# Long convolution on one core: the signal folded twice, and fewer weight tiles for its transform

## The chip, the cores and the metric

The kernel runs on one core of a Trainium2 chip. The metric is the device time of one launch in microseconds (us), the median of several executions. Five engines work side by side, each on its own list of instructions: TensorE (PE, matrix products), VectorE (DVE), ScalarE (ACT), GpSimd (POOL) and SyncE (SP, which issues most DMAs). They meet at semaphores only.

## The reference

The reference is a two-layer language model block (gated recurrence, windowed attention, feed-forward) followed by a second two-layer block on the same 512 positions and 1024 channels (latent attention, then a "hyena" layer). The change is in the hyena layer, whose core is a long convolution by Fourier transform:

```python
def fft_long_conv(u, spec):
    L = u.shape[1]                                  # 512 positions
    U = jnp.fft.rfft(u.astype(jnp.float32), n=2 * L, axis=1)
    return jnp.fft.irfft(U * spec, n=2 * L, axis=1)[:, :L].astype(u.dtype)

def hyena_seq(t, w_in, conv_w, conv_b, spec, bias, w_out):
    u, gate = jnp.split(t @ w_in, [(HY_ORDER + 1) * HY_WIDTH], axis=-1)
    u = depthwise_conv(u, conv_w, conv_b)           # width 3
    v, *gates = jnp.split(u, HY_ORDER + 1, axis=-1)
    z = v
    for o in range(HY_ORDER):                       # 2 convolutions
        z = gates[o] * (fft_long_conv(z, spec[:, o]) + z * bias[o])
    return (z * jax.nn.silu(gate)) @ w_out
```

`spec` is the spectrum of a filter that is computed from small weights, once per launch.

## The kernel before

**Precision and weights.** Every product is made of three matmuls of the fast float type: high part by high part, high by low, low by high (`mm_w`, lines 322 to 328; `mm_x` at 330 with the operands exchanged). A tile is one 128x128 piece of a weight matrix; with 512 columns of data it costs three matmuls (L324, L327, L328). All weights of the launch come as one stream of chunks, 8 tiles each (512 KB). For each chunk SP loads `raw`, ACT writes the high part `whi` (L1196) and DVE the low part `wlo` (L1879). There are 4 buffers of `raw` and 3 of `whi` and `wlo` (`RAW, HL = 4, 3`).

**Where the splits stand.** The tiles are counted in order by `Tiles.take` on TensorE and by `Ahead.tiles` (L1173) in the programs of ACT and DVE. When the count passes the seventh tile of chunk c (`self.n % 8 == 6`), ACT and DVE place the split of chunk c + 2 at that point of their own lists. So the number of tiles that a stage takes sets not only TensorE's work but also *between which of their other instructions* ACT and DVE make the splits of that stage and of all stages behind it. TensorE waits for the `wlo` of a chunk at the chunk's first tile.

**The hyena layer** (from about 1640 us of the span on) works on halves of the channels, c = 0 and 1 (4 blocks `ct` of 128 channels each), and on two convolutions, od = 0 and 1. The order is: projections (`channels`), turn(0,0), convolve(0,0), projections and turn(1,0), convolve(1,0), projections of the second half and turn(0,1), convolve(0,1), projections and turn(1,1), convolve(1,1), output projection. Pairs in brackets are (od, c).

- `turn(od, c)` folds the signal in time. DVE writes, for each block ct, the sum and the difference of positions t and 511 - t (L2590 and L2592, 256 columns each) to `zf`. TensorE transposes 16 pieces of `zf` (L1035), four at a time (t = 0 to 3); each group of four reads all four blocks, so the first group waits for DVE's last fold. ACT and DVE take each group out as `zh` (L1774) and `zl` (L2597). This is woven into the projections by fixed counts (`weave`), the same counts on all engines.
- `convolve(od, c)` has four steps `forward(j)`, one for each group of 128 frequencies, and four `inverse(j)`, in the order forward 0, forward 1, inverse 0, forward 2, inverse 1, forward 3, inverse 2, inverse 3. A forward takes two tiles for the filter's real part (PSUM bank `bk`), two for its imaginary part (`bj`), for j = 0 two more (`alt`), then two for the signal's real part (`bu`, from the sums) and two for its imaginary part (`bi`, from the differences): 10 tiles for j = 0, 8 for the others. The signal's tiles are those named `mdft`.
- Behind each forward DVE makes four products (L2617, L2620, L2621, L2624), POOL the difference of the first two (L2782) and DVE the sum of the others (L2626); ACT takes the high parts (`yh`, L1816), DVE the low parts (`yl`, L2629). An inverse takes 4 tiles with half the columns (24 matmuls at L331, L334, L335) and waits for `yl`.
- For j = 0 ACT and DVE mend row 0 of the filter's spectrum (L1809, then `hl_h` at L2611), and forward(1) waits for it on TensorE (`made_v "hm"`, line 1069).
- Behind inverse(3) DVE makes four results of each of four blocks (L2650, L2651, L2654, L2657) and only then the next split.

The lines of `convolve` on TensorE that take the signal's tiles:

```python
for k in range(2):
    w = tiles.take([("mdft", k, j)])
    ...
    op = mm_w(bu, w, a.zh[:, k, :], a.zl[:, k, :], k == 0, k == 1)
op.then_inc(*s.filled.tick("bu", od, c, j))
```

Of the kernel before, what the change touches and what calls it, by code (L numbers as in the profile page):

```python
# [13 lines left out]
MUL, ADD, SUB = ALU.mult, ALU.add, ALU.subtract  # L14
# [300 lines left out]
def tensor_program(e, m, s):  # L315
    q = Waits(e)
# [653 lines left out]
    def hyena():  # L970
        a = m.hy
# [83 lines left out]
        def convolve(od, c):  # L1055
            y = a.y[od, c]
            bu, bk, bi, bj = B[4:8]
            prev = (0, c) if od else (1, 0) if c else None

            def forward(j):  # L1060
                sums, differences = (0, 1), (2, 3)
                for k, x in enumerate(sums if j < 2 else differences):
                    w = tiles.take([("dft", k, j)])
                    if k == 0:
                        if j:
                            q.wait_ge(*s.taken_a.at("bk", od, c, j - 1))
                        else:
                            q.wait_ge(*(s.taken_a.at("bk", *prev, 3) if prev else s.h.at("mla_out", 2)))
                        q.wait_ge(*(s.made_v.at("hm", od, c) if j else s.made_v.at("h_lo", od, c, 0)))
                    op = mm_w(bk, w, a.hh[:, 0, x, :], a.hl[:, 0, x, :], k == 0, k == 1)  # L1070
                op.then_inc(*s.filled.tick("bk", od, c, j))
                for k, x in enumerate(differences if j < 2 else sums):
                    w = tiles.take([("dft", k, 4 + j)])
                    if k == 0:
                        q.wait_ge(*(s.taken_a.at("bj", od, c, j - 1) if j else s.made_v.at("zt", od, c, 3)))
                        q.wait_ge(*s.made_v.at("h_lo", od, c, 3))
                    op = mm_w(bj, w, a.hh[:, 1, x, :], a.hl[:, 1, x, :], k == 0, k == 1)
                op.then_inc(*s.filled.tick("bj", od, c, j))
                if j == 0:
                    for k, x in enumerate(sums):  # L1080
                        w = tiles.take([("alt", k, 0)])
                        if k == 0:
                            q.wait_ge(*s.taken_a.at("bk", od, c, 0, "first"))
                        op = mm_w(bk, w, a.hh[:, 0, x, :], a.hl[:, 0, x, :], k == 0, k == 1)
                    op.then_inc(*s.filled.tick("alt", od, c))
                for k in range(2):
                    w = tiles.take([("mdft", k, j)])
                    if k == 0 and j:
                        q.wait_ge(*s.taken_v.at("bu", od, c, j - 1))
                    elif k == 0:  # L1090
                        q.wait_ge(*(s.taken_v.at("bu", *prev, 3) if prev else s.h.at("mla_out", 1)))
                    op = mm_w(bu, w, a.zh[:, k, :], a.zl[:, k, :], k == 0, k == 1)
                op.then_inc(*s.filled.tick("bu", od, c, j))
                for k in range(2):
                    w = tiles.take([("mdft", k, 4 + j)])
                    if k == 0 and j:
                        q.wait_ge(*s.taken_v.at("bi", od, c, j - 1))
                    op = mm_w(bi, w, a.zh[:, 2 + k, :], a.zl[:, 2 + k, :], k == 0, k == 1)
                op.then_inc(*s.filled.tick("bi", od, c, j))

            def inverse(j):
                i = j % 2
                for p in range(2):
                    hi, lo, old = tiles.take([("idft", j, 2 * p + x) for x in range(2)])
                    half = slice(256 * p, 256 * p + 256)
                    q.wait_ge(*s.made_v.at("y_lo", od, c, j, p))
                    for ct in range(4):
                        cs = slice(128 * ct, 128 * ct + 128)
                        if j == 0 and p == 0:
                            if od == 0:  # L1110
                                q.wait_ge(*s.taken_a.at("conv", 8 + 4 * c + ct))
                            elif ct < 2:
                                q.wait_ge(*s.taken_a.at("conv", 16 + 4 * c + ct + 2))
                            else:
                                q.wait_ge(*s.taken_v.at("hg", c, ct))
                        op = mm_x(B[ct][:, half], (hi, lo), y.hi[:, i, p, cs], y.lo[:, i, p, cs], j == 0 and p == 0,
                                  j == 3, old if ct == 0 else None, skip=True)
                        if j == 3 and p == 1 and ct < 3:
                            op.then_inc(*s.valued.tick("inv", od, c, ct))
                op.then_inc(*s.valued.tick("ydone", od, c, j))  # L1120

            forward(0)
            for j in range(1, 4):
                forward(j)
                if j == 3 and (od, c) != (1, 1):
                    for x in range(2):
                        tiles.mark(("rows", *((0, 1) if od else (1, c)), x), x)
                inverse(j - 1)
            inverse(3)
            if od == 1 and c == 1:  # L1130
                for gen in begun:
                    for _ in range(4):
                        next(gen)
# [53 lines left out]
def scalar_program(e, m, s, A, chunks):  # L1187
    q = Waits(e)
# [9 lines left out]
    w = Ahead(split_hi, chunks)  # L1198
# [519 lines left out]
    def hyena():  # L1718
        a = m.hy
# [57 lines left out]
        def convolve(od, c):  # L1777
            y = a.y[od, c]
            bu, bk, bi, bj = B[4:8]
            ks, tmp = m.sqb, a.tmp  # L1780

            def forward(j):
# [16 lines left out]
                if j == 0:  # L1799
# [7 lines left out]
                    e.activation(a.alt[:, :], bk, ACT.Copy).then_inc(*s.taken_a.tick("bk", od, c, 0))  # L1807
                    q.wait_ge(*s.made_v.at("row 0", od, c))
                    e.activation(a.hh[0:1, 0, 0, :], a.hm[0:1, :], ACT.Copy).then_inc(*s.made_a.tick("hm", od, c))  # L1809
                for _ in range(4):  # L1810
                    w.tiles(1)
                for p, name in enumerate(("yr", "spec")):
                    q.wait_ge(*(s.made_v if p else s.made_p).at(name, od, c, j))
# [58 lines left out]
def vector_program(e, m, s, chunks):  # L1872
    q = Waits(e)
# [671 lines left out]
    def hyena():  # L2545
        a = m.hy
# [39 lines left out]
        def turn(od, c):  # L2586
            zf = a.zf[2 * c + od]
            for ct in range(4):
                q.wait_ge(*(s.made_v.at("inv", 0, c, ct) if od else s.made_v.at("conv", 4 * c + ct)))
                e.tensor_tensor(zf[:, ct, 0:256], z[:, ct, 0:256], z[:, ct, 511:255:-1],  # L2590
                                ADD).then_inc(*s.made_v.tick("zf0", od, c, ct))
                e.tensor_tensor(zf[:, ct, 256:512], z[:, ct, 0:256], z[:, ct, 511:255:-1],  # L2592
                                SUB).then_inc(*s.made_v.tick("zf", od, c, ct))
                yield
            for t in range(4):
# [4 lines left out]
        def convolve(od, c):  # L2600
# [3 lines left out]

            def forward(j):
                i = j % 2
                for _ in range(10 if j == 0 else 8):
                    w.tiles(1)
                if j == 0:
                    q.wait_ge(*s.made_a.at("hm", od, c))  # L2610
# [324 lines left out]
def fourier():  # L2935
# [14 lines left out]
    ic[0, :] = 1 / 1024  # L2950
    isn[0, :] = -alt / 1024
    cat = lambda a, b: np.concatenate([a, b], 1).astype(np.float32)
    return cat(c, s), c2.astype(np.float32), cat(mc, ms), cat(ic, isn)


def filter_tables():
# [131 lines left out]
```

## Time and profile before

| what | value |
|---|---|
| median of 3 runs | 2037.94 us (2037.1 to 2038.3) |
| span of the profiled execution | 2037.5 us, 0.4 us below the median |
| PE busy | 1978.4 us, 97% |
| DVE busy | 1380.5 us, 68% |
| ACT busy | 828.0 us, 41% |
| mean granted clock of TensorE | 0.988 of full |

TensorE is busy nearly all the time, so its idle stretches and the number of its matmuls tell most of the time. The busy share of DVE is a mean: in the hyena layer it is higher in some stretches than in others, and there it can be what TensorE waits for. A matmul's duration in the trace is its latency; the distance between two starts is its cost in a row of them.

### The profile page before, as it was taken

To read this page: it belongs to the slowest core of one execution; us is meant where nothing else is said; L and a number is where in the kernel's file an instruction comes from. 1 tells how busy PE (TensorE), PEld (TensorE's weight loads), DVE (VectorE), ACT (ScalarE), POOL (GpSimd) and SP (SyncE) were. 2 spreads that over 40 slices of the span, in tenths; PEclk is the share of its full clock that TensorE was granted. 3 is DMA by queue.
4 is the path that set the end of the run, shared out by engine and by line. 5 is a ranking of instruction groups with operands and counts; after the bars stand their busy time and mean duration, and the time that the engine had idled before them with its cause. 6 is when DMAs were issued, how large, how long until landed. Compare 5 with 4: busy or idle time off the path is not lost.

```text
span 2037.5 us, 24678 instructions
## 1 busy us (share of the span) xinstructions
PE 1978.4 (97%) x9878; PEld 1655.8 (81%) x9878; DVE 1380.5 (68%) x1961; ACT 828.0 (41%) x1259; POOL 233.3 (11%) x234
## 2 busy tenths in 40 slices
PE   8999999999999999999999999999999989999997
PEld 6888887788888888888888888778888878888786
DVE  5577765997789667756764784555555567787774
ACT  5233334442233245544432443444344444454442
POOL 2132231003201230010000001000000101000011
PEclk9999999999999999999999999999999989999998
DMA  5211112345534341114344333311111323232421
GB/s 182 72 56 54 61 53 85 130 150 179 201 138 157 132 137 34 40 64 147 137 159 135 126 133 99 108 62 42 42 32 42 114 73 124 93 126 81 145 94 52
DMA packets 60963, 208.40 MB, mean 102 GB/s; under 512 B 6832, under 2 KB 7152, under 8 KB 59696
## 3 DMA queue, kind: packets, MB, share of 16 engines
q1 hardware_dynamic: 53296, 193.19, 27.9%
q10 hardware_dynamic: 7552, 13.64, 1.9%
q8 instruction: 78, 1.28, 0.2%
q14 instruction: 37, 0.30, 0.0%
HBM read 196.31 MB, written 10.49 MB: 101 GB/s over the span
## 4 chain that ended last, share of the span: by engine, by line
PE 79%; DVE 13%; ACT 5%; issue 2%; POOL 1%; DMA 0%; ACTq 0%; DVEq 0%; SPq 0%
PE PS L324 21%; PE PS L328 20%; PE PS L327 20%; DVE wlo L1879 2%; PE PS L436 2%; PE PS L933 2%; PE PS L331 1%; PE PS L335 1%; PE PS L334 1%; ACT whi L1196 1%; PE PS L922 1%; PE PS L685 1%; PE PS L386 1%; PE PS L726 1%; DVE col_f L2094 1%
## 5 line engine op out<-in xcount | busy, mean ns | idle before, releaser
L324 PE MATMUL PS<-nhi,whi 128*128 128x512 f32 x1456 | 593.1, 407 | 15.4 <-DVE wlo L1879 3.7
L328 PE MATMUL PS<-nhi,wlo 128*128 128x512 f32 x1456 | 571.8, 393 | 0.0
L327 PE MATMUL PS<-nlo,whi 128*128 128x512 f32 x1456 | 570.6, 392 | 0.0
L1879 DVE TENSOR_TENSOR wlo<-raw,whi 128x1024 fp32r<-128x1024 f32 x291 | 368.4, 1276 | 176.5 <-ACT whi L1196 175.4
L1196 ACT ACTIVATE whi<-raw 128x1024 fp32r<-128x1024 f32 x291 | 303.3, 1052 | 209.0 <-PE PS L324 133.2
L324 PEld LDWEIGHTS PS<-nhi,whi 128*128 128x128 f32 x1456 | 276.1, 190 | 78.4 <-issue 11.3
L328 PEld LDWEIGHTS PS<-nhi,wlo 128*128 128x128 f32 x1456 | 275.3, 189 | 59.7
L327 PEld LDWEIGHTS PS<-nlo,whi 128*128 128x128 f32 x1456 | 276.4, 190 | 53.5 <-issue 2.6
L2723 POOL TENSOR_TENSOR diag<-diag,sqb 128x512 f32<-128x512 f32 (+1 forms) x56 | 73.6, 1314 | 780.9 <-ACT sqb L1205 698.3
L324 PE MATMUL PS<-hh_f,whi 128*128 128x512 f32 x352 | 137.8, 392 | 0.0
L327 PE MATMUL PS<-hl_f,whi 128*128 128x512 f32 x352 | 137.7, 391 | 0.0
L328 PE MATMUL PS<-hh_f,wlo 128*128 128x512 f32 x352 | 137.5, 391 | 0.0
L2739 POOL TENSOR_TENSOR sd_f<-ab_f 128x512 f32<-128x512 f32 x32 | 55.3, 1745 | 271.7 <-DVE ab_f L2182 271.1
L2094 DVE SCALAR_TENSOR_TENSOR col_f<-aw_f,scv,col_f 128x1024 f32<-128x1024 f32 x63 | 85.0, 1358 | 0.0
L328 PEld LDWEIGHTS PS<-hh_f,wlo 128*128 128x128 f32 x352 | 66.5, 189 | 14.0
L324 PEld LDWEIGHTS PS<-hh_f,whi 128*128 128x128 f32 x352 | 66.4, 189 | 13.9
L327 PEld LDWEIGHTS PS<-hl_f,whi 128*128 128x128 f32 x352 | 66.5, 189 | 13.7
L1419 ACT ACTIVATE t_f<-gp_f,par 128x512 f32<-128x512 f32 x44 | 35.9, 816 | 94.3 <-DVE gp_f L2199 94.3
L1665 ACT ACTIVATE pt_m<-PS 128x768 f32<-128x768 f32 x32 | 25.9, 811 | 111.8 <-PE PS L922 111.8
L1923 DVE TENSOR_TENSOR hT<-hT,PS 128x512 f32<-128x512 f32 x48 | 32.8, 682 | 52.2 <-PE PS L328 52.1
L436 PEld LDWEIGHTS PS<-qa,kk 128*128 128x128 f32 x448 | 56.0, 191 | 14.2 <-DVE qa L2031 10.3
L1205 ACT ACTIVATE sqb<-hT 128x512 f32<-128x512 f32 x42 | 26.3, 629 | 94.7 <-DVE hT L1923 62.5
(356 smaller groups left out, 3373.2 us busy)
## 6 DMA issues: line engine op xcount, KB each, us to landing
raw<-in_stream SPq DMA_DIRECT2D x291, 512.0 KB, 3.5
aw_f<-in_ada SPq DMA_DIRECT2D x48, 512.0 KB, 4.4
rows<-sd_f ACTq DMA_DIRECT2D x32, 256.0 KB, 2.2
rows_h<-rows SPq DMA_DIRECT2D x8, 1024.0 KB, 6.1
wd_f<-in_decay ACTq DMA_DIRECT2D x16, 256.0 KB, 3.0
hT<-in_xT SPq DMA_DIRECT2D x8, 256.0 KB, 6.9
out<-hT SPq DMA_DIRECT2D x8, 256.0 KB, 2.0
wd_f<-in_filt_out ACTq DMA_DIRECT2D x8, 128.0 KB, 2.9
```

The costliest lines, as they stand in the source:

```text
L324: op = e.matmul(out, hi, xh, start=first, stop=False)
L327: e.matmul(out, hi, xl, start=False, stop=False)
L328: return e.matmul(out, lo, xh, start=False, stop=last)
L436: op = e.matmul(B[b][:, cs], kk[:, z, cs], qx[:, cs], start=True, stop=True)
L933: op = e.matmul(B[6][:, 128 * blk:128 * blk + 128], a.v[:, t, 128 * h:128 * h + 128], a.pt[:, i, 128 * t:128 * t + 128], start=t == 0, sto ...
L1196: e.activation(m.whi[:, c % HL, :], m.raw[:, c % RAW, :], ACT.Copy).then_inc(*s.w_hi.tick(c))
L1419: e.activation(a.t[:, 0, z, :], a.gp[:, z, 2:T + 2], ACT.Identity, bias=pc(cb, f), scale=pc(cw, 44 + f)).then_inc(*s.made_a.tick("c0", lay ...
L1879: e.tensor_tensor(m.wlo[:, c % HL, :], m.raw[:, c % RAW, :], m.whi[:, c % HL, :].bitcast(F), SUB).then_inc(*s.w_lo.tick(c))
L1923: op = e.tensor_tensor(h, h, B[b], ADD)
L2094: e.scalar_tensor_tensor(col[:, v, :], aw[:, n % AW[layer], :], m.scv[:, 2, k, v:v + 1], col[:, v, :], MUL, ADD).then_inc(*s.made_v.tick(" ...
L2723: e.tensor_tensor(acc, acc, m.sqb[:, i % 2 if site != "n4" else 0, 0:width], ADD).then_inc(*s.acc.tick(site, i))
L2739: e.tensor_tensor(a.sd[:, x, :], a.ab[:, 0, :], a.ab[:, 1, :], SUB if x else ADD).then_inc(*s.made_p.tick("sd", n, i, x))
```

## The change

The time-folded signal (256 rows of sums, 256 of differences) is folded once more, about the middle of its 256 rows. Of the four frequency groups the first two (every fourth frequency from 0, and from 2) have cosines and sines that are even or odd about that middle, so one half of the rows' contribution vanishes. For j = 0 and j = 1 the real and the imaginary part of the signal then take one tile each and not two. For j = 2 and 3 nothing is saved. The matrix `mdft` is folded on the host in the same way and scaled by 1/2. On DVE each block ct of a turn has two folds more: the first pair writes `zs` (in the buffer `sqb`), and a second pair, which waits for the first, writes `zf`.

```diff
+Z_SIGNS = [((0,), (1,)), ((1,), (0,)), ((0, 1), (0, 1)), ((0, 1), (0, 1))]
+Z_TILES = [2, 2, 4, 4]
...
-                for k in range(2):
+                for k in even:
                     w = tiles.take([("mdft", k, j)])
...
+                    op = mm_w(bu, w, a.zh[:, k, :], a.zl[:, k, :], k == even[0], k == even[-1])
...
-                for k in range(2):
+                for k in odd:
                     w = tiles.take([("mdft", k, 4 + j)])
...
-                for _ in range(4):
+                for _ in range(Z_TILES[j]):
                     w.tiles(1)
...
-                e.tensor_tensor(zf[:, ct, 0:256], z[:, ct, 0:256], z[:, ct, 511:255:-1],
+                e.tensor_tensor(zs[:, 0:256], z[:, ct, 0:256], z[:, ct, 511:255:-1],
+                                ADD).then_inc(*s.made_v.tick("zs0", od, c, ct))
+                e.tensor_tensor(zs[:, 256:512], z[:, ct, 0:256], z[:, ct, 511:255:-1],
+                                SUB).then_inc(*s.made_v.tick("zs1", od, c, ct))
+                q.wait_ge(*s.made_v.at("zs1", od, c, ct))
+                e.tensor_tensor(zf2[:, :, 0, :], zs2[:, :, 0:128], zs2[:, :, 255:127:-1],
                                 ADD).then_inc(*s.made_v.tick("zf0", od, c, ct))
-                e.tensor_tensor(zf[:, ct, 256:512], z[:, ct, 0:256], z[:, ct, 511:255:-1],
+                e.tensor_tensor(zf2[:, :, 1, :], zs2[:, :, 0:128], zs2[:, :, 255:127:-1],
                                 SUB).then_inc(*s.made_v.tick("zf", od, c, ct))
...
-                for _ in range(10 if j == 0 else 8):
+                for _ in range(Z_TILES[j] + (6 if j == 0 else 4)):
                     w.tiles(1)
...
+    folded = lambda a: np.concatenate([(a[0:128] + a[255:127:-1]) / 2, (a[0:128] - a[255:127:-1]) / 2], 0)
+    return cat(c, s), c2.astype(np.float32), cat(folded(mc), folded(ms)), cat(ic, isn)
```

A convolution thus takes 46 tiles and not 50, the launch 289 chunks and not 291. Counted from convolve(0,0), which starts at the first tile of a chunk, the four convolutions start at tile 0, 2, 4 and 6 of a chunk before the change and at 0, 6, 4 and 2 after it.

The first place where instructions move is turn(1,1) on DVE, in the projections ahead of the last convolution. `zf<-z_h` is a fold, `sqb<-z_h` and `zf<-sqb` are the first and second folds of the new code, `wlo` is the split of a chunk. Before:

```order
L1879 TENSOR_TENSOR wlo<-raw,whi 128x1024
L2590 TENSOR_TENSOR zf<-z_h 128x256
L2592 TENSOR_TENSOR zf<-z_h 128x256
L2590 TENSOR_TENSOR zf<-z_h 128x256
L2592 TENSOR_TENSOR zf<-z_h 128x256
L2580 SCALAR_TENSOR_TENSOR rb<-rb,PS 128x512
L2583 SCALAR_TENSOR_TENSOR g_h<-g_h,rb 128x512
L1879 TENSOR_TENSOR wlo<-raw,whi 128x1024
```

The same place after the change:

```order
L2599 TENSOR_TENSOR sqb<-z_h 128x256
L2601 TENSOR_TENSOR sqb<-z_h 128x256
L2604 TENSOR_TENSOR zf<-sqb 128x2x128
L2606 TENSOR_TENSOR zf<-sqb 128x2x128
L1882 TENSOR_TENSOR wlo<-raw,whi 128x1024
L2599 TENSOR_TENSOR sqb<-z_h 128x256
L2601 TENSOR_TENSOR sqb<-z_h 128x256
L2604 TENSOR_TENSOR zf<-sqb 128x2x128
L2606 TENSOR_TENSOR zf<-sqb 128x2x128
L2583 SCALAR_TENSOR_TENSOR rb<-rb,PS 128x512
L2586 SCALAR_TENSOR_TENSOR g_h<-g_h,rb 128x512
```

Each block has four folds now, and the split stands between the first and the second block, where it stood ahead of both before.

The second place is DVE at the start of convolve(1,1). `rb` and `g_h` are the last gate of the projections, `hl_h` is the mended row. Before:

```order
L2580 SCALAR_TENSOR_TENSOR rb<-rb,PS 128x512
L2583 SCALAR_TENSOR_TENSOR g_h<-g_h,rb 128x512
L1879 TENSOR_TENSOR wlo<-raw,whi 128x1024 x2
L2611 TENSOR_TENSOR hl_h<-rb,hh_h 1x512
L2617 TENSOR_TENSOR tmp_h<-PS,sqb 128x512
```

After:

```order
L2583 SCALAR_TENSOR_TENSOR rb<-rb,PS 128x512
L2586 SCALAR_TENSOR_TENSOR g_h<-g_h,rb 128x512
L1882 TENSOR_TENSOR wlo<-raw,whi 128x1024
L2625 TENSOR_TENSOR hl_h<-rb,hh_h 1x512
L2631 TENSOR_TENSOR tmp_h<-PS,sqb 128x512
```

One split stands ahead of the mended row and not two; the other has moved behind the step's products.

## Rows read from the trace of the kernel before

**Rows 1.** What TensorE waited for, 1655 us to the end: total us, times, longest
```profile
PE PS L331 <- DVE yl L2629: 4.3, 4, 1.5
PE PS L324 <- DVE hl_h L2611: 2.8, 2, 1.4
PE PS L324 <- DVE wlo L1879: 2.8, 2, 2.1
```

**Rows 2.** Timeline of TensorE, convolve(0,0): start, us, engine, line, operation [idle before]
```profile
1693.46 0.39 PE L324 MATMUL PS<-zh_h,whi 128*128 128x512 f32 x1
...
1695.95 0.39 PE L328 MATMUL PS<-zh_h,wlo 128*128 128x512 f32 x1
1697.78 0.47 PE L324 MATMUL PS<-hh_h,whi 128*128 128x512 f32 x1 [1.44 <-DVE hl_h L2611]
...
1720.02 0.28 PE L331 MATMUL PS<-whi,yh 128*128 128x256 f32 x1
...
1722.77 0.28 PE L335 MATMUL PS<-whi,yl 128*128 128x256 f32 x1
```

**Rows 3.** Timeline of VectorE, turn(0,0), and two results behind convolve(0,0)
```profile
1671.00 0.42 DVE L2590 TENSOR_TENSOR zf<-z_h 128x256 f32<-128x256 f32 x1
1671.33 0.42 DVE L2592 TENSOR_TENSOR zf<-z_h 128x256 f32<-128x256 f32 x1
...
1675.93 0.42 DVE L2592 TENSOR_TENSOR zf<-z_h 128x256 f32<-128x256 f32 x1
...
1727.16 0.41 DVE L2651 TENSOR_TENSOR tmp_h<-PS,sqb 128x256 f32<-128x256 f32 x1
1727.61 0.75 DVE L2654 SCALAR_TENSOR_TENSOR tmp_h<-z_h,par,tmp_h 128x512 f32<-128x512 f32 x1
```

**Rows 4.** Timeline of all engines, ends of the four turns: last folds, first transposes
```profile
1677.26 0.60 PE L1035 MATMUL PS<-ident,zf 128*128 128x128 f32 x4
...
1755.01 0.65 PE L1035 MATMUL PS<-ident,zf 128*128 128x128 f32 x4
...
1844.60 0.75 DVE L2557 SCALAR_TENSOR_TENSOR tmp_h<-up_h,par,tmp_h 128x512 f32<-128x512 f32 x1 [0.75 <-ACT tmp_h L1740]
...
1846.50 0.69 PE L1035 MATMUL PS<-ident,zf 128*128 128x128 f32 x4
...
1917.03 0.69 DVE L2580 SCALAR_TENSOR_TENSOR rb<-rb,PS 128x512 f32<-128x512 f32 x1 [0.75 <-ACT rb L1763]
...
1920.51 0.42 DVE L2592 TENSOR_TENSOR zf<-z_h 128x256 f32<-128x256 f32 x1
1921.65 0.60 PE L1035 MATMUL PS<-ident,zf 128*128 128x128 f32 x4
```

**Rows 5.** Timeline of VectorE, the first step of convolve(0,0)
```profile
1697.56 0.67 DVE L2617 TENSOR_TENSOR tmp_h<-PS,sqb 128x512 f32<-128x512 f32 x1
1698.16 0.67 DVE L2620 TENSOR_TENSOR tmp_h<-PS,sqb 128x512 f32<-128x512 f32 x1
...
1700.89 1.29 DVE L2629 TENSOR_TENSOR yl<-tmp_h,yh 128x512 fp32r<-128x512 f32 x2
1703.37 1.23 DVE L1879 TENSOR_TENSOR wlo<-raw,whi 128x1024 fp32r<-128x1024 f32 x1 [1.18 <-ACT whi L1196]
1704.51 0.68 DVE L2617 TENSOR_TENSOR tmp_h<-PS,sqb 128x512 f32<-128x512 f32 x1
```

**Rows 6.** Timeline, last step of convolve(1,1), and TensorE behind convolve(0,1)
```profile
1901.11 0.50 PE L324 MATMUL PS<-nhi,whi 128*128 128x512 f32 x1 [2.05 <-DVE wlo L1879]
...
1971.48 0.68 DVE L2620 TENSOR_TENSOR tmp_h<-PS,sqb 128x512 f32<-128x512 f32 x1
...
1974.97 0.39 PE L331 MATMUL PS<-whi,yh 128*128 128x256 f32 x1 [1.55 <-DVE yl L2629]
```

**Rows 7.** Stretches: PE, PEld, DVE, ACT, POOL busy (x), PEclk, DMA share, GB/s
```profile
1322.00:1324.00 2.00, 0.21 (x1) 0.24 (x2) 0.79 (x2) 2.00 (x5) 0.57 (x1) 1.00 0.00 0
1572.00:1574.00 2.00, 1.08 (x3) 0.89 (x4) 1.97 (x5) 0.00 (x0) 0.00 (x0) 0.50 0.00 0
```

More of the change, by code:

```diff
@@ L1085, in forward @@
                     op.then_inc(*s.filled.tick("alt", od, c))
-                for k in range(2):
-                    w = tiles.take([("mdft", k, j)])
[L1088 to L1092, printed above, removed]
+                even, odd = Z_SIGNS[j]
+                if j:
+                    q.wait_ge(*s.taken_v.at("bu", od, c, j - 1))
+                else:
+                    q.wait_ge(*(s.taken_v.at("bu", *prev, 3) if prev else s.h.at("mla_out", 1)))
+                for k in even:
+                    w = tiles.take([("mdft", k, j)])
+                    op = mm_w(bu, w, a.zh[:, k, :], a.zl[:, k, :], k == even[0], k == even[-1])
                 op.then_inc(*s.filled.tick("bu", od, c, j))
-                for k in range(2):
+                if j:
+                    q.wait_ge(*s.taken_v.at("bi", od, c, j - 1))
+                for k in odd:
                     w = tiles.take([("mdft", k, 4 + j)])
-                    if k == 0 and j:
-                        q.wait_ge(*s.taken_v.at("bi", od, c, j - 1))
-                    op = mm_w(bi, w, a.zh[:, 2 + k, :], a.zl[:, 2 + k, :], k == 0, k == 1)
+                    op = mm_w(bi, w, a.zh[:, 2 + k, :], a.zl[:, 2 + k, :], k == odd[0], k == odd[-1])
                 op.then_inc(*s.filled.tick("bi", od, c, j))
@@ L2588, in turn @@
             for ct in range(4):
+                zs = m.sqb[:, ct % 2, :]
+                zs2, zf2 = zs.rearrange("p (a t) -> p a t", a=2), zf[:, ct, :].rearrange("p (a b t) -> p a b t", a=2, b=2)
                 q.wait_ge(*(s.made_v.at("inv", 0, c, ct) if od else s.made_v.at("conv", 4 * c + ct)))
-                e.tensor_tensor(zf[:, ct, 0:256], z[:, ct, 0:256], z[:, ct, 511:255:-1],
+                if od == 0 and c == 0:
+                    q.wait_ge(*s.sums.at("n5"))
+                elif ct < 2:
+                    q.wait_ge(*s.made_v.at("inv", *((0, c) if od else (1, 0)), 3))
+                e.tensor_tensor(zs[:, 0:256], z[:, ct, 0:256], z[:, ct, 511:255:-1],
[4 more added lines that the diff above has]
+                e.tensor_tensor(zf2[:, :, 0, :], zs2[:, :, 0:128], zs2[:, :, 255:127:-1],
                                 ADD).then_inc(*s.made_v.tick("zf0", od, c, ct))
-                e.tensor_tensor(zf[:, ct, 256:512], z[:, ct, 0:256], z[:, ct, 511:255:-1],
+                e.tensor_tensor(zf2[:, :, 1, :], zs2[:, :, 0:128], zs2[:, :, 255:127:-1],
                                 SUB).then_inc(*s.made_v.tick("zf", od, c, ct))
@@ L2952, in fourier @@
     cat = lambda a, b: np.concatenate([a, b], 1).astype(np.float32)
-    return cat(c, s), c2.astype(np.float32), cat(mc, ms), cat(ic, isn)
+    folded = lambda a: np.concatenate([(a[0:128] + a[255:127:-1]) / 2, (a[0:128] - a[255:127:-1]) / 2], 0)
+    return cat(c, s), c2.astype(np.float32), cat(folded(mc), folded(ms)), cat(ic, isn)
 def filter_tables():
```

## The prediction, on record before the kernel ran

> **What bounds the kernel now.** I read the list of TensorE's waits first, because TensorE is busy nearly throughout: whatever it does not wait for costs only what its own matmuls cost. In the hyena layer it waits 4.3 us in four waits for `yl`, 2.8 us in two for `hl_h`, 2.8 us in two for `wlo` [rows 1]: each time for VectorE. Then the timeline of TensorE in one convolution, for the price of a tile: from 1693.46 to 1695.95 lie 11 distances between matmul starts, 0.226 us each, so a tile (three matmuls) costs 0.68 us [rows 2]. Then VectorE's timeline in the turns and in the steps of a convolution, to see how much room it has. In the turns it has little; that decides the case.
>
> **Removed on TensorE.** Two tiles in forward(0) and two in forward(1), four convolutions: 16 tiles, 16 x 0.68 = 10.9 us if TensorE alone set the pace. With them go two chunks, with their loads and splits; nothing waited for the loads, and the splits' time is within what follows.
>
> **Added on VectorE, the turns.** A pair of folds is 0.33 us from start to start, 1671.00 to 1671.33 [rows 3]. The second pair waits for the first's last result. What such a wait costs stands at L2651 to L2654: 0.45 us from start to start where 0.33 would do, so 0.12 more [rows 3]. A block gets 2 x 0.33 + 0.12 = 0.79 us more, a turn 4 x 0.79 = 3.2 us. The new form (2 x 128 columns, read backwards) is not in this trace. The nearest row is the old fold, also 256 columns with one operand backwards, and I take it; the upper bound is the pitch of an instruction of 512 columns, 0.60 us from 1697.56 to 1698.16 [rows 5], which would make 8 x 0.27 = 2.1 us more in a turn, 8.5 us in all. A gain is excluded, as the elements are no fewer.
>
> TensorE's first transposes read the last fold, so I take off the room of each turn:
> - turn(0,0): the last fold ends at 1675.93 + 0.42 = 1676.35; the fourth transpose, which reads it, starts a quarter us behind 1677.26 [rows 3, 4]. Room 1.2, new wait 2.0 us.
> - turn(1,0): its splits now fall as those of turn(1,1) did before, since its projections start at the same tile of a chunk (the sixth). There the last fold ends at 1920.93 and the fourth transpose starts at 1921.9: room 1.0, and VectorE stood idle 0.75 us among the folds at 1917.03 [rows 4]. New wait 3.2 - 1.0 - 0.75 = 1.4 us.
> - turn(0,1): same order as before. Its four transposes take 0.69 us where those of 1677.26 take 0.60: they wait already. Idle 0.75 at 1844.60 [rows 4]. New wait 2.4 us.
> - turn(1,1): takes the order that turn(1,0) had. There the transposes at 1755.01 take 0.65 us, so they wait already [rows 4], and VectorE works without a gap of note from the end of the convolution on. New wait 3.2 us.
>
> Together 9.0 us of new waits. Behind the transposes stand the matmuls of the projections in TensorE's list, so nothing fills them. Later waits do not absorb them either: the whole chain to `hl_h` starts from TensorE's own `alt` product.
>
> **Moved: the split behind a convolution.** VectorE makes 16 results behind inverse(3) before the next split. Where the convolution ends at the sixth tile of a chunk, TensorE has 10 tiles of cover and then waits: 2.05 us at 1901.11, behind convolve(0,1) [rows 6]. Convolutions ended at tile 2, 4, 6, 0 of a chunk, and now end at 6, 4, 2, 0. The wait moves from convolve(0,1) to convolve(0,0): +2.05 - 2.05 = 0.
>
> **The convolutions.** Two tracks run side by side. TensorE's, from the release by `hl_h`: 6 tiles of forward(1), then twice an inverse (24 matmuls from 1720.02 to 1722.77, so 2.9 us [rows 2]) and 8 tiles. VectorE's: a step of products, sum and low parts is 4.6 us from 1697.56 to the end of `yl` at 1702.18, and each split adds 1.15 us [rows 5] and, where ScalarE makes the high half behind its `yh`, 0.2 to 1.2 us of waiting. At the end stands a fixed chain, L2620 at 1971.48 to inverse(3) at 1974.97, 3.5 us [rows 6]. I laid both tracks with the new order of the splits:
> - convolve(0,0): TensorE waited 1.44 us for `hl_h` at 1697.78 [rows 2], and the chain to `hl_h` starts ahead of the signal's tiles. So forward(0)'s two tiles (1.36 us) only lengthen the wait. Forward(1)'s 1.36 is gained, and 0.6 of the last wait, because no split stands ahead of the last products now: 2.0.
> - convolve(1,0): `hl_h` has no split just ahead of it and comes 6.1 us behind the start; TensorE is ready at 5.4 and waits 0.7. After that TensorE sets the pace: 1.9.
> - convolve(0,1): the same start; in the last step two splits stand ahead of the products, which come 0.6 us later than TensorE: 1.3.
> - convolve(1,1): VectorE and ScalarE also make `nlo` and `nhi`. Forward(1) starts 1.8 us earlier (one split less ahead of `hl_h`, as the second order piece shows), but VectorE's steps then last 7.5, 7.1 and 8.6 us, as long as before, and the last wait grows from 1.55 to some 3.2 us: 1.4.
>
> Gained together 6.6 us of the 10.9. The bounds of this term are 2 x 1.36 = 2.7 us (only the two forwards(1) in which nothing but TensorE worked) and 10.9 us.
>
> **The clock.** TensorE now waits five times for 2.7 to 3.2 or for 2.0 to 2.4 us. The trace shows both outcomes: an idle stretch of that size at 1322 us with the granted clock at 1.00, and 0.50 (1.2 GHz where 1.00 is 2.4 GHz) at 1572 us behind two idle stretches [rows 7]. A fall costs half of the time for which it lasts while TensorE is the bound. I take one fall that costs 1.2 us; bounds 0 and 5. The Trainium skill (TensorE: Matmul & The Clock Gate, Why this matters for your kernels) says the same of idle gaps between bursts of matmuls, as a rule against making them; the trace agrees at 1572 us and not at 1322 us. [...]
>
> **Sum.** The profiled execution spans 2037.5 us: + 9.0 - 6.6 + 0 + 1.2 = + 3.6, that is 2041.1. The median of the runs lies 0.4 above it: 2041.5 us. I call 0.2% (4.1 us, to 2033.9 and 2042.0) the bound below which a measurement of this kernel tells no change. So: no change, but close to slower.
>
> **Rivals.**
> 1. Slower by the clock: the new waits of 2.0 to 3.2 us, all in front of stretches where TensorE is the bound, bring its clock down three or four times. Against it speaks the stretch at 1322 us, of the same size, which left the clock at 1.00 [rows 7]. From two falls on the kernel is measurably slower; with four, 5 us: 2037.9 + 2.4 + 5 = 2045.3. Chance 0.2.
> 2. No fall of the clock: 2037.9 + 9.0 - 6.6 = 2040.3. Chance 0.3.
> 3. The convolutions give all of the 10.9 us, as TensorE's share of busy time suggests: 2037.9 + 9.0 - 10.9 = 2036.0. Against it: four waits for `yl` and two for `hl_h` show that VectorE's track is already the longer one at places. Chance 0.1.
> 4. Faster: the folds find room that I do not see and the turns cost nothing. 2037.9 - 10.9 = 2027.0, or 2031.3 with 6.6. Against it: the transposes wait already in two turns of four. Chance 0.05.
> 5. The new form of fold costs like 512 columns: 8.5 more, 2050. Chance 0.03, since columns set the time in all rows of VectorE that I read.
>
> The forecast itself has 0.32. Range: 2037.5 to 2045. Below it lie rivals 3 and 4, above it 5. Slower than 2042.0 are rivals 1 and 5 nearly whole and four tenths of the forecast's own scatter (1.5 us to either side): 0.38. Faster than 2033.9: rival 4 and a little of 3: 0.06. Within: 0.56.
>
> **What would show it.** In the changed kernel TensorE's waits list a new entry, transposes (L1035) behind VectorE's second folds, four times, some 9 us together and over 3 us the longest. The wait for `wlo` of 2 us stands behind convolve(0,0) and not (0,1). The wait for `yl` ahead of the last inverse of convolve(1,1) is near 3 us. A second fold is 0.33 us behind the one ahead of it. The waits for `hl_h` are 2.8 us in convolve(0,0) and below 1 in the others. The slices of the granted clock show whether it fell behind 1690 us. The prediction is wrong if the transposes wait less than 6 us together, or if the hyena layer's convolutions are shortened by over 9 us.

## The result, and the profile after

The changed kernel takes 2045.54 us (median of 5 runs, 2045.26 to 2045.86), the kernel before 2037.89 us beside it (5 runs, 2035.19 to 2038.3): ratio 1.0036, 95% interval 1.0023 to 1.0048. It is slower, by 7.7 us. The forecast was 2041.5 us, its range ended at 2045.0, and "slower" had a chance of 0.38.

The list of TensorE's waits from 1655 us on in the changed kernel (total us, times, longest), against [rows 1]:

```profile
PE PS L1037 <- DVE zf L2606: 7.6, 6, 2.3
PE PS L333 <- DVE yl L2643: 5.4, 4, 2.7
PE PS L326 <- DVE hl_h L2625: 5.0, 4, 2.8
PE PS L326 <- DVE wlo L1882: 2.8, 2, 2.1
```

The transposes are new in the list with 7.6 us. The waits for `hl_h` grew from 2.8 to 5.0 us and those for `yl` from 4.3 to 5.4; those for `wlo` are as they were. Where they stand is in the timeline of TensorE (start, us, operation [idle before <- releaser]), picked rows of the changed kernel:

```profile
1675.13 0.33 PE L1037 MATMUL PS<-ident,zf 128*128 128x128 f32 x1 [0.49 <-DVE zf L2606]
1676.60 0.33 PE L1037 MATMUL PS<-ident,zf 128*128 128x128 f32 x1 [1.14 <-DVE zf L2606]
...
1698.41 0.76 PE L326 MATMUL PS<-hh_h,whi 128*128 128x512 f32 x1 [2.79 <-DVE hl_h L2625]
...
1736.88 0.50 PE L326 MATMUL PS<-nhi,whi 128*128 128x512 f32 x1 [2.05 <-DVE wlo L1882]
...
1851.16 0.33 PE L1037 MATMUL PS<-ident,zf 128*128 128x128 f32 x1 [2.21 <-DVE zf L2606]
...
1924.64 0.33 PE L1037 MATMUL PS<-ident,zf 128*128 128x128 f32 x1 [0.31 <-DVE zf L2606]
1927.25 0.48 PE L1037 MATMUL PS<-ident,zf 128*128 128x128 f32 x1 [2.27 <-DVE zf L2606]
...
1979.80 0.38 PE L333 MATMUL PS<-whi,yh 128*128 128x256 f32 x1 [2.70 <-DVE yl L2643]
```

These are turns (0,0), (0,1) and (1,1), `hl_h` and `wlo` in and behind convolve(0,0), and `yl` ahead of the last inverse. Turn (1,0) has a wait of 1.14 us at 1759.09. The wait for `wlo` that stood at 1901.11 [rows 6] now stands at 1736.88. The last row answers to the 1.55 us at 1974.97 [rows 6].

The folds themselves, VectorE's timeline of the changed kernel in turn(0,0), against [rows 3]:

```profile
1668.00 0.42 DVE L2599 TENSOR_TENSOR sqb<-z_h 128x256 f32<-128x256 f32 x1
1668.34 0.42 DVE L2601 TENSOR_TENSOR sqb<-z_h 128x256 f32<-128x256 f32 x1
1668.79 0.43 DVE L2604 TENSOR_TENSOR zf<-sqb 128x256 f32<-128x256 f32 x1
1669.13 0.42 DVE L2606 TENSOR_TENSOR zf<-sqb 128x256 f32<-128x256 f32 x1
```

The new form costs what the old one does: 0.42 us, starts 0.34 us apart and 0.45 where it waits for the one ahead (0.33 and 0.45 in [rows 3]).

Then the granted clock, read in stretches of 2 us from 1650 to 1995 us. Busy times stand first, the clock (PEclk) is the third number from the end; five places of the changed kernel:

```profile
1676.00:1678.00 2.00, 1.40 (x6) 1.17 (x7) 2.00 (x4) 0.60 (x1) 0.00 (x0) 0.87 0.00 0
1678.00:1680.00 2.00, 2.00 (x6) 1.42 (x5) 1.70 (x3) 0.00 (x0) 0.00 (x0) 0.50 0.47 131
1680.00:1682.00 2.00, 2.00 (x10) 1.81 (x9) 0.29 (x1) 0.92 (x2) 0.00 (x0) 0.78 0.32 131
1698.00:1700.00 2.00, 1.59 (x4) 1.33 (x5) 2.00 (x5) 0.00 (x0) 0.46 (x1) 0.50 0.66 147
1852.00:1854.00 2.00, 2.00 (x7) 1.50 (x6) 0.84 (x2) 0.12 (x1) 0.00 (x0) 0.50 0.32 43
1928.00:1930.00 2.00, 2.00 (x6) 1.60 (x5) 1.14 (x2) 1.51 (x3) 0.00 (x0) 0.50 0.32 129
1982.00:1984.00 2.00, 2.00 (x12) 2.00 (x11) 0.33 (x1) 0.00 (x0) 0.00 (x0) 0.50 0.34 53
```

Each place stands at one of the waits above: of 1.14 (with 0.49 us just ahead), 2.79, 2.21, 2.27 and 2.70 us. The clock falls between 0.6 us ahead of the wait's end (at 1926.6, where the wait ends at 1927.25) and 1.5 us behind it (at 1981.3, where it ends at 1979.80). What a fall costs is worked out from the first three rows: 2 x (0.13 + 0.50 + 0.22) = 1.7 us of TensorE's time. All stretches below 1.00 between 1650 and 1995 us together make 8.5 us, five times 1.7. I call this sum the clock's loss. It is an upper bound of what the falls cost, since two of them begin while TensorE still waits, which is some 0.5 us of the 8.5. In the trace of the kernel before the loss is 0; three long stretches of it:

```profile
1690.00:1727.00 37.00, 34.30 (x194) 29.79 (x194) 27.25 (x38) 17.31 (x28) 5.17 (x4) 1.00 0.33 113
...
1811.00:1860.00 49.00, 48.26 (x220) 39.56 (x219) 38.38 (x54) 24.99 (x34) 0.00 (x0) 1.00 0.32 103
...
1897.00:1945.00 48.00, 45.95 (x211) 37.74 (x210) 34.92 (x48) 23.07 (x32) 0.00 (x0) 1.00 0.29 90
```

The account: 16 tiles, -10.9; transposes, +7.6; `hl_h`, +2.2; `yl`, +1.1; clock, +8.5. Sum +8.5 us, where the medians differ by 7.7. The two traces themselves differ by 9.2 us from turn(0,0)'s first fold to the end: 366.5 us (from 1671.00, span 2037.5) and 375.7 us (from 1668.00, span 2043.7). Ahead of that fold the code is the same, and yet the changed kernel was 3.0 us quicker there, with 13.7 us of loss between 400 and 1650 us against 18.8.

So the clock also falls where nothing was changed, and not in each execution. One place shows it best: near 1323 us TensorE waits 2.63 us for VectorE in all 14 profiled kernels of this document, with the same code up to there. In 10 of them, the kernel before among them, the clock stays at 1.00; in four (e2, e4, e9 and e11 below) it falls. Here are e9's rows:

```profile
1324.01 0.76 PE L325 MATMUL PS<-nhi,whi 128*128 128x512 f32 x1 [2.63 <-DVE call L2378]
1324.00:1326.00 2.00, 1.99 (x5) 1.61 (x6) 1.50 (x2) 2.00 (x4) 1.86 (x2) 0.50 0.00 0
```

The loss of a profile is therefore that of one execution. The mean granted clock is known for every execution and gives an estimate of the loss over the whole span, (1 - clock) x span: a mean of 28.6 us for the changed kernel (5 executions) and 22.2 to 23.0 us for the kernel before (22, 24 and 14 executions beside the experiments), so some 6 us more.

### The profile page after: what moved, and what is told of

The parts are those of the page before. It is cut to its first block, busy times and chain, and to the rows that moved or that the text cites. A ratio compares the mean times of both kernels' runs of the same rounds, so it can differ in the third digit from the quotient of the medians.

```text
span 2043.7 us, 24605 instructions
## 1 busy us (share of the span) xinstructions
PE 1973.1 (97%) x9830; PEld 1649.3 (81%) x9830; DVE 1390.0 (68%) x1991; ACT 827.2 (40%) x1257; POOL 233.7 (11%) x234
## 4 chain that ended last, share of the span: by engine, by line
PE 75%; DVE 16%; ACT 5%; issue 3%; POOL 1%; DMA 0%; ACTq 0%; DVEq 0%; SPq 0%
PE PS L326 19%; PE PS L330 19%; PE PS L329 19%; DVE wlo L1882 3%; PE PS L438 2%; PE PS L935 2%; PE PS L333 1%; PE PS L337 1%; PE PS L336 1%; ACT whi L1199 1%; PE PS L924 1%; PE PS L687 1%; PE PS L388 1%; PE PS L728 1%; DVE col_f L2097 1%
```

## The experiments

All times are medians of 5 to 11 runs; each ratio is to the kernel before on the same chip, with its 95% interval. It goes by all executions and is not the quotient of two medians; the medians of the kernel before beside the experiments were 2037.3 to 2039.5 us. "Loss" is the clock's loss between 1650 and 1995 us as above, in the one profiled execution.

| run | time, us | ratio | waits: transposes / hl_h / yl / wlo | loss |
|---|---|---|---|---|
| before | 2037.89 | 1 | - / 2.8 / 4.3 / 2.8 | 0 |
| changed | 2045.54 | 1.0036 [1.0023, 1.0048] | 7.6 / 5.0 / 5.4 / 2.8 | 8.5 |
| e1_folds_only | 2049.61 | 1.0055 [1.0042, 1.0068] | 7.8 / 2.8 / 4.3 / 2.7 | 6.8 |
| e2_tiles_only | 2032.67 | 0.9970 [0.9958, 0.9983] | - / 5.0 / 5.4 / 2.7 | 3.4 |
| e3_fill | 2037.81 | 1.0001 [0.9992, 1.0009] | 0.7 / 2.2 / 2.7 / 2.8 | 1.7 |
| e4_hm_first | 2041.41 | 1.0018 [1.0009, 1.0027] | 7.5 / 2.9 / 5.9 / 2.8 | 6.8 |
| e6_pool_folds | 2046.18 | 1.0040 [1.0027, 1.0052] | 8.8 / 5.0 / 5.4 / 2.8 | 5.1 |
| e7_early | 2043.06 | 1.0023 [1.0014, 1.0032] | 9.2 / 5.0 / 5.4 / 0.7 | 5.1 |
| e8_all | 2043.68 | 1.0021 [1.0013, 1.0030] | 10.6 / 2.9 / 5.9 / 0.6 | 5.1 |
| e9_before_both | 2033.87 | 0.9974 [0.9963, 0.9984] | - / - / 5.2 / 0.7 | 1.7 |
| e10_later | 2032.94 | 0.9975 [0.9966, 0.9985] | 0.8 / 5.0 / 5.4 / 2.8 | 1.7 |
| e11_later_all | 2029.26 | 0.9957 [0.9944, 0.9969] | 1.1 / 2.9 / 5.9 / 0.7 | 3.4 |
| e12_out_first | 2029.39 | 0.9958 [0.9945, 0.9970] | 1.2 / 2.9 / 3.2 / 0.7 | 1.7 |
| e13_before_three | 2032.48 | 0.9972 [0.9960, 0.9984] | - / - / 5.2 / 0.7 | 1.7 |

**The two halves of the change.** The folds alone, with all tiles taken as before:

```diff
-Z_SIGNS = [((0,), (1,)), ((1,), (0,)), ((0, 1), (0, 1)), ((0, 1), (0, 1))]
-Z_TILES = [2, 2, 4, 4]
+Z_SIGNS = [((0, 1), (0, 1))] * 4
+Z_TILES = [4, 4, 4, 4]
```

> The changed kernel with the second folds on VectorE, but all four frequency groups take both tiles again, so 50 tiles in a convolution and the splits where they stood before the change. Theory A (the new waits ahead of the transposes, and TensorE's clock falling behind them): waits for the folds of 2.0, 3.2, 2.4 and 1.4 us, together 9 us, and three or four falls of the granted clock at 1.5 us each: 2037.9 + 9 + 5 = 2052 us. Theory B (waits alone, no clock): 2047 us. Theory C (the folds are hidden and the loss came from the moved splits): within 1 us of before.

The fewer tiles alone, with VectorE's old pair of folds in place of the two pairs (the signal of groups 0 and 1 is then not folded the second time):

```diff
-                e.tensor_tensor(zs[:, 0:256], z[:, ct, 0:256], z[:, ct, 511:255:-1],
...
+                e.tensor_tensor(zf[:, ct, 0:256], z[:, ct, 0:256], z[:, ct, 511:255:-1],
...
+                e.tensor_tensor(zf[:, ct, 256:512], z[:, ct, 0:256], z[:, ct, 511:255:-1],
```

> The changed kernel with one pair of folds for a block as before (so the signal that enters groups 0 and 1 is not folded a second time and the output differs), but with 46 tiles in a convolution. Theory A: the convolutions give 6.6 us, the wait for the low half of the weights moves from behind convolve(0,1) to behind convolve(0,0) at no cost, and the long waits for the mended row in convolve(0,0) (2.8 us) and for the low parts in convolve(1,1) (2.7 us) may each bring the clock down once, 1.5 us: 2031 to 2034.5 us. Rival (TensorE sets the pace): all 10.9 us, 2027. Rival (VectorE sets the pace in the convolutions): under 3 us gained, 2035 or more.

The folds alone cost 12.1 us (2049.61 against 2037.55 beside it), the tiles alone give 4.9. Together 7.2, against 7.7 measured: the halves add, as far as intervals of 2.5 us to either side can tell. The folds' 12.1 is 7.8 us of waits at the transposes and the rest, 4.3, by inference the clock (3.6 by the mean clock of all executions, 25.8 us of loss against 22.2); its profiled execution lay 4.2 us above its median, so its loss of 6.8 (three falls, one of them twice as long as the others and worth 3.4) is high for it. Its waits for `hl_h` and `yl` are those of the kernel before. The tiles' 10.9 us shrink by 2.2 (`hl_h`), 1.1 (`yl`) and two falls (3.4), to 4.2; measured 4.9.

**The clock by itself.** TensorE's idle time ahead of six waits is filled with matmuls whose result is overwritten; no wait of the chain goes away by it.

```diff
+FILL = {(0, 0): 7, (1, 0): 5, (0, 1): 9, (1, 1): 11, "hm": 12, "yl": 9}
...
+        def fill(bank, n, x=None):
+            x = m.nhi[:, 0, :] if x is None else x
+            for _ in range(n):
+                e.matmul(bank, x[:, 0:128], x, start=True, stop=True)
```

> The changed kernel with matmuls without use put on TensorE in front of six of its waits: 7, 5, 9 and 11 ahead of the first transposes of turns (0,0), (1,0), (0,1), (1,1), 12 ahead of forward(1) of convolve(0,0), 9 ahead of the last inverse of convolve(1,1), about as long as the waits. They shorten no wait. Theory A (the clock falls behind idle stretches and costs some 1.4 us for each of five falls): granted clock 1.00 through the hyena layer up to its last stage, and 2045.5 - 7 = 2038.5 us. Theory B (the clock has no part in the loss): 2045.5 us or a little more.

2037.81 us, 7.7 less than the changed kernel: the time of the kernel before. TensorE's timeline of this kernel in turn(0,0) shows the seven fillers in place of the wait:

```profile
1673.21 1.75 PE L1023 MATMUL PS<-nhi 128*128 128x512 f32 x7
1674.80 0.49 PE L1045 MATMUL PS<-ident,zf 128*128 128x128 f32 x3
1675.53 0.33 PE L1045 MATMUL PS<-ident,zf 128*128 128x128 f32 x1 [0.24 <-DVE zf L2619]
1675.62 0.48 PE L327 MATMUL PS<-nhi,whi 128*128 128x512 f32 x1
```

The fourth transpose still comes when its fold is done, but the matmuls 1 us behind it take 0.39 us, where those of the changed kernel take 0.63, and the granted clock is 1.00 in this kernel all the way from 1667 to 1690 us. The loss went from 8.5 to 1.7 us, that is by 6.8: all five falls are gone and one came, behind the 2.07 us wait for `wlo`, which has none in the changed kernel. By the mean clock of all executions the loss went from 28.6 to 20.0 us. This is the run that prices the clock, since useful work and order are the same: 7.7 us of time for four falls fewer in the profile.

**The mended row.** In forward(0) VectorE makes `hl_h` ahead of the split that stands between, not behind it.

```diff
-                for _ in range(Z_TILES[j] + (6 if j == 0 else 4)):
-                    w.tiles(1)
+                more = Z_TILES[j] + (6 if j == 0 else 4)
                 if j == 0:
+                    for _ in range(6):
+                        w.tiles(1)
+                    more -= 6
...
+                for _ in range(more):
+                    w.tiles(1)
```

> The changed kernel with the mended row's low part on VectorE placed ahead of the split that falls in the signal's tiles of forward(0); only in convolve(0,0) does this change the order. Theory A: the wait for it falls from 2.79 to 0.9 us, the clock does not fall behind it, and both are kept: 2045.5 - 3.3 = 2042.2 us. Rival: VectorE's later steps take the time back (its products wait for the split all the same): the wait for the low parts ahead of the last inverse grows by 1.9 us, and only the clock's 1.4 us are gained or nothing: 2044 to 2045.5 us.

Waits for `hl_h` fell from 5.0 to 2.9 us, those for `yl` grew by 0.5, and the time fell by 4.1 where the theory had 3.3. The fall of the clock at 1698 us is gone, but one at 1736 came, behind the `wlo` wait that had not brought one before. The fall at 1982 is gone too, though the wait for `yl` of 2.70 us there is as it was.

**The second folds on GpSimd.** Blocks 0 to 2 of each turn.

```diff
+                if ct == 3:
+                    q.wait_ge(*s.made_v.at("zs1", od, c, ct))
...
+    def turn(od, c):
+        for ct in range(3):
...
+            q.wait_ge(*s.made_v.at("zs1", od, c, ct))
+            for x in range(2):
+                e.tensor_tensor(zf2[:, :, x, :], zs2[:, :, 0:128], zs2[:, :, 255:127:-1],
+                                SUB if x else ADD).then_inc(*s.made_p.tick("zf" if x else "zf0", od, c, ct))
```

> The changed kernel with the second pair of folds of blocks 0 to 2 of each turn on GpSimd; only block 3's stay on VectorE. Theory (the new folds on VectorE make the transposes late, 7.6 us in six waits, and the falls of the clock follow these waits): the transposes' waits fall to 1.5 us or less together, the clock no longer falls behind a turn (1688, 1863 and 1938 us before), and the time falls by some 6 us of waits and 3 to 4 us of clock, from 2045.5 to about 2036. Rival 1 (GpSimd needs longer for a fold of 256 columns than VectorE has between two blocks, so VectorE or TensorE waits for GpSimd instead): the waits stay above 5 us with GpSimd's folds as their releaser, 2043 or more. Rival 2 (the clock falls by the waits for hl_h and yl as often as before): about 2039 to 2040.

The first rival holds: 2046.18 us, and the transposes wait 8.8 us, 6.4 of it for GpSimd. (Its loss of 5.1 us is that of one execution; by the mean clock of all of them it lost 28.6 us, as the changed kernel did.) GpSimd's timeline in turn(0,0), each row two folds:

```profile
1671.57 2.53 POOL L2808 TENSOR_TENSOR zf<-sqb 128x256 f32<-128x256 f32 x2 [41.16 <-DVE sqb L2603]
1674.46 2.33 POOL L2808 TENSOR_TENSOR zf<-sqb 128x256 f32<-128x256 f32 x2 [0.36 <-DVE sqb L2603]
1677.48 1.70 POOL L2808 TENSOR_TENSOR zf<-sqb 128x256 f32<-128x256 f32 x2 [0.69 <-DVE sqb L2603]
```

And VectorE's at the same time:

```profile
1670.74 0.42 DVE L2601 TENSOR_TENSOR sqb<-z_h 128x256 f32<-128x256 f32 x1
1671.07 0.42 DVE L2603 TENSOR_TENSOR sqb<-z_h 128x256 f32<-128x256 f32 x1
1671.41 1.22 DVE L1882 TENSOR_TENSOR wlo<-raw,whi 128x1024 fp32r<-128x1024 f32 x1
1672.55 0.96 DVE L2601 TENSOR_TENSOR sqb<-z_h 128x256 f32<-128x256 f32 x1
1673.43 0.95 DVE L2603 TENSOR_TENSOR sqb<-z_h 128x256 f32<-128x256 f32 x1
```

The same fold takes VectorE 0.42 us while GpSimd is idle and 0.96 us while it works, and GpSimd's fold takes 0.74 us at the shortest and 1.66 at the longest of 24. So the work moved off VectorE comes back on it: in turn(0,0) five of its folds are longer by 2.5 us together, and the six that moved away had taken it 2.4.

**The split behind a convolution earlier.**

```diff
-            w.upto(w.n // 8 + 1)
+            w.upto((w.n + AHEAD[od, c]) // 8 + 1)
```

(`AHEAD` is 4 for the first three convolutions and 0 for the last, on ScalarE and VectorE.)

> The changed kernel with the first split behind a convolution placed ahead of some of VectorE's and ScalarE's results of that convolution, where it stood behind all of them. Theory (the wait for wlo at 1736.9 and 1820.4 us is an instruction order, 2.05 and 0.73 us): both waits go, and the time falls by 2 to 3 us, to 2042.5 to 2043.5. Rival (the results that now come later make the next turn's folds later by the split's 1.15 us, and the transposes wait longer by as much): the wait for wlo goes, the transposes' waits in turns (1,0) and (0,1) grow by 1 us each, and the time stays at 2045.

2043.06 us. The wait for `wlo` of 2.05 us is gone and one of 0.7 remains, but the transposes wait 1.6 us more: both the theory and the rival are at work, the time is where the theory put it.

**Both edits, with GpSimd's folds.**

> The changed kernel with three edits together: second folds of three blocks on GpSimd, the split behind a convolution earlier, and the mended row hl_h ahead of the split. If the three costs are separate, the time is that of the changed kernel less the sum of the three gains (hl_h alone gave 4.1 us): 2045.5 - 9 - 2.5 - 4.1 = about 2030. If they share the falls of the clock, so that the same fall was counted in each, 2032 to 2034. If the work only moves to the wait for yl at the end of the convolutions, 2036 or more.

2043.68 us. The sum of the gains is wrong by 14 us, because e6 gives no gain where 9 us were put in. The number of the last case, 2036 or more, is met, but not its cause: the wait for `yl` is 5.9 us against 5.4, while the transposes wait 10.6. It contains the edits of e4, e6 and e7.

**The kernel before with the edits of e4 and e7.**

> The kernel before with the two edits that do not need the second fold: hl_h ahead of the split, and the split behind a convolution earlier. It tells what the change is worth when the kernel that it is set against has lost the same waits. Theory (hl_h 2.8 us and wlo 2.8 us of waits, of which the wait for yl takes some back): 2037.9 - 2 to 4 = about 2035, so that the changed kernel with all edits (about 2030 to 2033) stays 2 to 5 us ahead by its 16 fewer tiles. Rival (the edits are worth nearly all that the changed kernel gains): 2032 or less.

2033.87 us, as expected. It has no wait for `hl_h` left.

**The transposes later.** TensorE's transposes stand one step of the interleaving further on; everything else is the changed kernel.

```diff
         def turn(od, c):
             zf = a.zf[2 * c + od]
-            for ct in range(4):
+            for ct in range(5):
                 yield
             for t in range(4):
```

> The changed kernel with TensorE's transposes of each turn placed one step of the interleaving later, 2.8 to 3.5 tiles of the projections; nothing changes on VectorE, ScalarE or GpSimd. Theory (the new folds only come late for where the transposes stand; they cost waits and falls of the clock, and no work of TensorE): the 7.6 us of waits at the transposes shrink to 1 us or less, the falls of the clock behind turns (0,0), (0,1) and (1,1) go with them (some 1.5 us each), and the time is 2045.5 - 6.6 - 4.5 = about 2034.5. Rival 1 (VectorE is the bound through the whole turn, and the wait moves to the first signal tiles of the convolution or to hl_h): the transposes' waits go, others grow by as much, 2040 to 2045. Rival 2 (the clock falls for another reason than these waits): 2039.

2032.94 us, 1.6 less than expected, and the interval is below 1. TensorE's waits in this kernel:

```profile
PE PS L333 <- DVE yl L2643: 5.4, 4, 2.7
PE PS L326 <- DVE hl_h L2625: 5.0, 4, 2.8
PE PS L326 <- DVE wlo L1882: 2.8, 2, 2.1
...
PE PS L1037 <- DVE zf L2606: 0.8, 1, 0.8
```

Three waits are as in the changed kernel to the tenth, so nothing else took the time over. And the clock (columns as above):

```profile
1676.00:1678.00 2.00, 2.00 (x11) 1.56 (x10) 1.97 (x3) 0.60 (x1) 0.00 (x0) 1.00 0.06 12
1678.00:1680.00 2.00, 2.00 (x12) 1.72 (x11) 1.53 (x3) 1.40 (x2) 0.00 (x0) 1.00 0.81 250
1694.00:1696.00 2.00, 2.00 (x5) 1.63 (x6) 2.00 (x4) 0.00 (x0) 0.92 (x1) 0.50 0.83 231
1852.00:1854.00 2.00, 2.00 (x12) 1.67 (x12) 1.72 (x2) 1.03 (x2) 0.00 (x0) 1.00 0.00 0
1928.00:1930.00 2.00, 2.00 (x12) 1.69 (x11) 0.69 (x1) 1.57 (x3) 0.00 (x0) 1.00 0.03 8
```

The falls behind the three turns are gone with their waits, and that behind `hl_h` is left. The fourth that is gone stood ahead of the last inverse, and its wait is still there, of 2.70 us as before:

```profile
1967.68 0.39 PE L333 MATMUL PS<-whi,yh 128*128 128x256 f32 x1 [2.70 <-DVE yl L2643]
1968.00:1970.00 2.00, 2.00 (x19) 2.00 (x18) 1.84 (x3) 0.95 (x1) 0.00 (x0) 1.00 0.00 0
```

So of the 6.8 us of loss that went, 5.1 went with their waits and 1.7 by the scatter of the falls. With the 6.8 us of waits that is 13.6 or 11.9; the medians say 12.6.

**The three orders together**, on the changed kernel:

> The changed kernel with three orders changed together, no work added or moved to another engine: the transposes one step later, hl_h ahead of the split, the split behind a convolution earlier. Theory: the gains add, as their waits are at different places: 2045.5 - 11 - 4.1 - 2.5 = 2028, and it is some 6 us ahead of the kernel before with the two edits that it can have (2033.9), since 16 tiles of 0.68 us are 10.9 and the wait for yl takes up to 5 of it. Rival (the wait for yl takes all that the tiles give once the other waits are gone): 2032 to 2034, no better than the kernel before with its two edits.

2029.26 us, ratio 0.9957: the fastest, level with the next run, and 3.7 us less than with the later transposes alone. The expectation was 2028. Its loss of 3.4 us is one fall of double length, at the wait for `yl` of 2.70 us.

**Output tiles ahead of the last inverse.**

```diff
+            if od == 1 and c == 1:
+                for _ in range(4):
+                    next(begun[0])
             inverse(3)
```

> The three orders of the run before it, and four tiles of the output projection ahead of the last inverse of convolve(1,1) on TensorE, where TensorE waits 2.7 us for yl. Theory (that wait is a gap that other work can fill, but these four tiles wait themselves for VectorE's products of the last step, which end about 2 us ahead of yl): 1 to 2 us less than with the three orders alone, and one fall of the clock fewer. Rival (the four tiles wait as long as the inverse does, because their bank comes free with the same chain): no change.

2029.39 us: no change, as the rival had it, though with 5 executions each a gain of 1 us could be missed. The wait for `yl` fell from 5.9 to 3.2 us, but the four tiles wait 1.9 us themselves, for the products that free their bank. That is less than the 2.7 us of the inverse and leaves 0.8 us that the medians do not show. (The profiled execution of e11 lay 3.8 us above its median and that of this kernel on it, so their losses of 3.4 and 1.7 us are not compared.)

**The fair opponent.** The kernel before with the same three orders as e11.

> The kernel before with all three orders: the transposes one step later, hl_h ahead of the split, the split behind a convolution earlier. It is the fair opponent of the changed kernel with the same three orders (2029.3, ratio 0.9957). Theory (the transposes of the kernel before hardly wait, so the later place gives it nothing; the 16 tiles are what differs): the time is that of the two orders alone, ratio 0.9974, 2033 to 2035, and the changed kernel is 3 to 5 us ahead of it. Rival (the later transposes help the kernel before as well, by the part of the wait that shows only as long transposes): ratio 0.996 or less, and the change is worth nothing even so.

2032.48 us, ratio 0.9972, as with two orders (0.9974): the kernel before gets nothing from later transposes. Against e11 the change is ahead by 0.0015 or some 3 us (5.4 by the medians against those of the kernel before beside them, 2039.46 and 2037.30), but the intervals (0.9944 to 0.9969 and 0.9960 to 0.9984) overlap, so that it is ahead at all is likely and not shown. e12 against e9 points the same way, 0.9958 and 0.9974.

## Why the prediction was wrong

**The clock: the step that failed.** "I take one fall that costs 1.2 us; bounds 0 and 5." There were five, 1.7 us each, 8.5 us together by the trace; e3, with four falls fewer, gives 7.7 us of time. Two things were mis-sized. The number: I weighed two stretches of the trace, one with the clock at 1.00 and one with 0.50 [rows 7], counted five waits of 2.0 to 3.2 us in the changed kernel, and let one of them bring a fall. Of its six largest idle places five did (2.79, 2.70, 2.27, 2.21, and 1.14 with 0.49 just ahead; not 2.05). Two of the five stand behind `hl_h` and `yl`, places where the kernel before waits 1.44 and 1.55 us [rows 2, 6] without a fall, so a wait that only grew has to be counted with the new ones. The price: 1.7 and not 1.2 us. The bound of 5 was too low for the same reasons.

The reading of [rows 7] is where this began: each of the two stretches was one execution's outcome and no property of its place. The one at 1322 us falls in 4 of the 14 profiles and the one at 1572 us in 6. Over all 14, TensorE has 34 idle places of 2.0 to 2.8 us between 1655 and 1995 us: 21 have a fall in them or within 2 us behind, 13 have none. Of 20 single places of 1.2 to 1.6 us none has one. By these counts five such waits make three falls, some 5 us, with both more and fewer possible. Why this kernel has five, and why its five executions lie within only 0.6 us of each other, stays open. Rival 1 named this mechanism and gave 2045.3 us, with a chance of 0.2. It had the time right from somewhat different parts: four falls of 1.25 on a base 2.4 us above the kernel before, where it was five of 1.7 on a base that did not move.

**The waits at the transposes.** Forecast 9.0 us (2.0, 1.4, 2.4, 3.2), measured 7.6 (1.6, 1.1, 2.2, 2.6 with 0.3 of it early). The order of the turns came out, each 0.2 to 0.6 us too high; that "over 3 us the longest" was wrong, it is 2.3. The prices of the folds were right: 0.34 and 0.45 us.

**The convolutions.** Forecast -6.6 of 10.9 us. By the waits it was -10.9 + 2.2 + 1.1 = -7.6. The signs at the places were right: `hl_h` 2.79 us in convolve(0,0) and 0.65, 0.65 and 0.93 in the others, `yl` 2.70 us ahead of the last inverse (forecast 3.2). So the first two terms made +2.4 in the forecast and about 0 here; it is the clock that made the rest.

**The split behind a convolution.** The wait moved from behind convolve(0,1) to behind convolve(0,0), 2.05 us at both places, as forecast.

**The base.** The forecast took the profiled execution for one 0.4 us under the median. In all later runs the device time is 1.8 or 1.9 us above the span, so that execution took 2039.3 us, 1.4 over the median. The forecast time itself was the median plus the sum and is not touched. But it holds the fall of the clock at 1572 us, which the trace of the changed kernel lacks, so it may be an execution that lost to the clock what others did not (18.8 us between 400 and 1650 us, against 13.7 to 18.8 in the others).

**The other rivals.** No fall: excluded by the trace. The convolutions give all 10.9 us: 7.6 by the waits, 4.9 in e2. The folds hidden for nothing: false as the kernel stands, and true once the transposes stand one step later (e10). Folds like 512 columns: false. (The chance of "slower", 0.38, adds up to 0.36 from the parts that the prediction names.)

## What to carry to other kernels

When a new operation makes a wait in front of an engine that is otherwise always busy, look first whether the waiting instruction can stand a few tiles later in its own list: here that one line turned 7.7 us slower into 5 us faster, with the same work. Price each idle place of TensorE of two to three microseconds as the wait and some two thirds of a fall of its clock (21 of 34 places here), which with a fall is nearly twice the wait, and count the places that exist already and grow. Do not take the outcome at one place in one profile for a rule. Moving work from VectorE to GpSimd needs a measurement with both at work.

## What the runs showed of the hardware

- A fall of the granted clock costs 1.7 us of TensorE's time here (3.4 in e11 and once in e1, where it lasts twice as long), and idle places of 1.6 to 2.8 us are enough for it. They do not decide it alone: the wait of 2.05 us at 1736.88 is followed by 1.00 in the changed kernel, and the same wait by 0.58 in e3 and 0.50 in e4; the wait for `yl` of 2.70 us ahead of the last inverse has a fall in 3 of 8 profiles, that for `hl_h` of 2.79 us in 5 of 5. What tells these apart was not settled.
- Matmuls without a use, in the idle time, keep the clock up: 7.7 us in e3.
- VectorE's and GpSimd's two-operand instructions slow each other: the fold of 256 columns takes VectorE 0.96 us and not 0.42 beside GpSimd, and GpSimd 0.74 to 1.66 us.
- Executions of one kernel differ by their falls: in e11 the spans go from 2025.1 us at a mean clock of 0.991 to 2031.2 at 0.987. A term of 1 to 2 us is therefore not read from two executions.
